# Differential attention: VectorE copies a job's values out between the two score maxima of the newest job

## The reference, cut to what matters

```python
def one_block(qi):
    s = jnp.einsum('bqhcd,bkhcd->bhcqk', qi, k).astype(jnp.float32) * scale
    p = jax.nn.softmax(s, axis=-1)
    a = p[:, :, 0] - lam * p[:, :, 1]
    return jnp.einsum('bhqk,bkhe->bqhe', a.astype(v.dtype), v)
```

## Time and profile before

| | us |
|---|---|
| runs shown (three) | 4294.61, 4308.23, 4309.19 |
| their median | 4308.23 |
| the profiled execution, its own time | 4303.0 |
| its span in the trace | 4300.9 |
| first scores of the heads start at | 3423.48 |
| last "square" of the heads ends at | 3579.61 |

### The profile page before, as it was taken

One profiled execution on the slowest core, in us unless ns is written; L12 is line 12 of the kernel. 1 busy time (PEld: TensorE's weight loads), 2 busy tenths in 40 slices (PEclk: granted clock), 3 DMA queues, 4 the chain that ended last, 5 costly groups with the idle time before them and its releaser, 6 DMA issues. The chain is left out here.

```text
span 4300.9 us, 75825 instructions
## 1 busy us (share of the span) xinstructions
PE 3759.1 (87%) x32214; PEld 2095.4 (49%) x32214; DVE 1533.8 (36%) x3723; ACT 1372.6 (32%) x2940; POOL 201.0 (5%) x193
## 2 busy tenths in 40 slices
PE   7998778777776998998988979999969988799997
PEld 4554566666665544564666533333345454333332
DVE  3011666666664103452256231111132183211112
ACT  2102334344433113442546222222235262222222
POOL 0000000000000001100200000000012000000000
PEclk9999799999998999999999989999979999899998
DMA  5223344444343110001110249999742103699996
GB/s 208 76 85 121 96 120 120 115 125 118 110 130 122 64 60 1 20 20 68 35 42 1 101 169 385 390 393 391 317 140 89 43 1 119 249 390 389 390 390 269
DMA packets 314586, 696.03 MB, mean 162 GB/s; under 512 B 169216, under 2 KB 195968, under 8 KB 289152
## 3 DMA queue, kind: packets, MB, share of 16 engines
q1 hardware_dynamic: 293024, 612.41, 40.0%
q0 software_dynamic: 14048, 53.49, 3.6%
q10 hardware_dynamic: 7168, 25.17, 1.5%
HBM read 624.94 MB, written 63.71 MB: 160 GB/s over the span
## 5 line engine op out<-in xcount | busy, mean ns | idle before, releaser
L202 PE MATMUL ps<-arena 128*128 128x512 f32 (+8 forms) x4620 | 1458.6, 479 | 95.6 <-ACT arena L1137 23.9
L202 PEld LDWEIGHTS ps<-arena 128*128 128x128 f32 (+5 forms) x4620 | 786.5, 190 | 707.1 <-issue 457.4
L2584 PE MATMUL ps<-arena 128*32 128x512 f32 x9216 | 1022.6, 596 | 31.1 <-DMA arena<-in_w 26.5
L2584 PEld LDWEIGHTS ps<-arena 128*32 128x32 f32 x9216 | 306.7, 110 | 649.0 <-issue 632.3
L620 PE MATMUL ps<-arena 64*64 64x64 f32 (+1 forms) x10624 | 463.9, 241 | 173.6 <-DVE arena L1194 62.8
L620 PEld LDWEIGHTS ps<-arena 64*64 64x64 f32 x10624 | 415.3, 146 | 255.2 <-issue 103.5
L2718 DVE COPY arena<-ps 128x384 f32<-128x384 f32 x64 | 35.7, 557 | 655.7 <-PE ps L2643 655.7
L208 PE MATMUL ps<-arena 128*128 128x128 f32 x1168 | 189.0, 296 | 83.6 <-DVE arena L3037 41.4
L2694 ACT ACTIVATE arena<-ps 96x512 f32<-96x512 f32 x64 | 38.0, 594 | 622.8 <-PE ps L2584 622.8
L208 PEld LDWEIGHTS ps<-arena 128*128 128x128 f32 x1168 | 140.3, 150 | 140.2 <-DVE arena L3037 44.9
L600 DVE SCALAR_TENSOR_TENSOR arena<-arena 128x769 f32<-128x769 f32 x48 | 45.7, 1015 | 275.9 <-PE ps L202 275.6
(11 more groups left out here) (282 smaller groups left out, 3769.4 us busy)
## 6 DMA issues: line engine op xcount, KB each, us to landing
arena<-in_w SPq DMA_DIRECT2D x192, 2048.0 KB, 30.6
arena<-in_w_mod SPq DMA_DIRECT2D x24, 2048.0 KB, 8.9
arena<-in_mod_w SPq DMA_DIRECT2D x12, 2048.0 KB, 9.4
yb<-arena ACTq DMA_DIRECT2D x64, 384.0 KB, 9.8
arena<-in_rwkv_w_in SPq DMA_DIRECT2D x8, 2048.0 KB, 10.0
arena<-rkvg SPq DMA_DIRECT2D x38, 384.0 KB, 4.2
rkvg<-arena POOLq DMA_DIRECT2D x32, 384.0 KB, 2.7
arena<-di SPq DMA_DIRECT2D x192, 64.0 KB, 2.5
```

Source lines behind the costliest of these rows:

```text
L202: ins = pe.matmul(out, l, r, start=(i == 0), stop=(i == len(pairs) - 1))
L2584: return pe.matmul(bank[32 * at:32 * at + 32, :], left[:, k, 32 * g:32 * g + 32], right[:, k, :], start=first, stop=last)
```

## The change

In DVE's order a round now has four pieces in place of three: the maximum for c = 0 of job r, "out" of job r-3, the maximum for c = 1 of job r, and "mix" of job r-1. No instruction is added or taken away, and none of ACT or PE moves. The semaphores count as before: `max` is counted by the maxima alone and `out` by "out" alone.

```diff
-        for what, n in self.rounds(((0, "max"), (3, "out"), (1, "mix"))):
+
+        for what, n in self.rounds(((0, 0), (3, "out"), (0, 1), (1, "mix"))):
...
-            elif what == "max":
-                for c in range(2):
-                    dve.wait_ge(self.scored, 2 * n + c + 1)
-                    dve.tensor_reduce(sm[:, c:c + 1], self.scores_at(n, c), AX.XY, ALU.max).then_inc(self.max, 1)
...
-            else:
+            elif what == "out":
                 dve.wait_ge(self.valued, n + 1)
                 dve.tensor_scalar(self.rows(n), self.values_at(n), sm[:, 4:5], None, ALU.mult).then_inc(self.out, 1)
+            else:
+                c = what
+                dve.wait_ge(self.scored, 2 * n + c + 1)
+                dve.tensor_reduce(sm[:, c:c + 1], self.scores_at(n, c), AX.XY, ALU.max).then_inc(self.max, 1)
```

More of the change, by code:

```diff
@@ L2505, in dve @@
                 dve.scalar_tensor_tensor(P0, P1, sm[:, 6:7], P0, ALU.mult, ALU.add).then_inc(self.mixed, 1)
-            elif what == "max":
-                for c in range(2):
-                    dve.wait_ge(self.scored, 2 * n + c + 1)
-                    dve.tensor_reduce(sm[:, c:c + 1], self.scores_at(n, c), AX.XY, ALU.max).then_inc(self.max, 1)
-                    dve.wait_ge(self.max, 4 * n + 2 * c + 1)
-                    dve.tensor_scalar(sm[:, c:c + 1], sm[:, c:c + 1], -self.SCALE, None, ALU.mult).then_inc(self.max, 1)
-            else:
+            elif what == "out":
                 dve.wait_ge(self.valued, n + 1)
                 dve.tensor_scalar(self.rows(n), self.values_at(n), sm[:, 4:5], None, ALU.mult).then_inc(self.out, 1)
+            else:
+                c = what
+                dve.wait_ge(self.scored, 2 * n + c + 1)
+                dve.tensor_reduce(sm[:, c:c + 1], self.scores_at(n, c), AX.XY, ALU.max).then_inc(self.max, 1)
+                dve.wait_ge(self.max, 4 * n + 2 * c + 1)
+                dve.tensor_scalar(sm[:, c:c + 1], sm[:, c:c + 1], -self.SCALE, None, ALU.mult).then_inc(self.max, 1)
     def over(self, e):
```

## The result

| | us |
|---|---|
| before, median of 20 runs | 4306.28 (4294.61 to 4314.16) |
| changed, median of 20 runs | 4319.62 (4309.90 to 4334.23) |
| ratio, with its 95% interval | 1.0035 (1.0026 to 1.0045) |
| span of the profiled execution, changed | 4321.8 |

The changed kernel is slower by 0.35%, some 15 us. The forecast was 4321 us.

A forecast was written before the change was run, and what follows sets the result against it. The prediction took a once-a-round loop through DVE, ACT and PE as the bound, 5.10 us against 4.58: -0.1 (first rounds) + 14.0 (27 rounds) + 1.3 (last) = 15.3 us slower, on 4305.6 giving 4321 us, range 4307 to 4331.

The forecast's parts named there:

- The loop: Out, second maximum, scaling, second exponential, square, turned, value, out, once a round: 5.10 us against 4.58, 14.0 lost in 27 rounds.
- The wait for "out" goes, and a longer one comes: PE no longer waits for "out" but about 1.0 us for ACT's copy before each value; DVE idles 1.2 before "out".
- the prediction's round of DVE, 3.89: DVE's instructions of one round added up without any wait: 3.89 us, shorter than the 5.10 us loop.
- Scores done before the copy: PE finishes its scores 2.49 us after "out" starts; the copy is ready for value only after 3.46.
- First rounds: Start of the heads: first "out" moves from 3438.79 to 3438.48; the second "out" comes 0.08 us earlier.
- Last rounds: After the last regular "out", the next value starts 3.46 us later instead of 2.15: 1.3 us lost.
- The clock rival: PE's clock falls in the rounds, each of 27 values pays 0.62 us, 16.7 us on top: 4338 us; chance 0.08.
- The faster rival: The copy does not bind and PE's loop sets the round: 15.4 us faster, 4290 us; chance 0.06.
- The level: Starting time to which the loss is added: middle of four executions, 4305.6 us, giving 4321 us.
- the band of 0.5%: What a measurement can tell from no change, 21.5 us; chance within it 0.76, slower 0.19, faster 0.05.
- The upper bound: A round costs between 0.48 and 0.60 us more, the whole 14 to 18 us; with the clock's placement 13 to 19.
- the rule of the Trainium skill: A Vector operation starts only once the previous one's pipe is empty: 27 x 0.08 = 2.2 us more; not adopted.

The follow-up runs named there:

- The 7.24 and 6.17 us rounds of one kernel: Kernel before, with DVE's "out" moved ahead of both maxima and ACT's order unchanged: median 4366.57 us, ratio 1.0152.
- 7.88 and 6.55 of another: Changed kernel, with DVE's "mix" also moved ahead of the second maximum and ACT's order unchanged: median 4369.41 us, ratio 1.0159.

## Why the prediction was right, and where it was off

- **The loop.** Its seven steps were added to 5.10 us from rows of the kernel before; the changed kernel has 5.11 or 5.12 in each of 27 rounds. Its steps as the round at 3495.45 shows them are 0.27, 0.98, 0.18, 0.90, 0.29, 0.85 and 1.64, none more than 0.01 from its term. The copy between the exponentials opens it, square ahead of them shortens it by its 0.29, mix in it lengthens it. This is shown, not only argued.
- **The wait for "out" goes, and a longer one comes.** PE waits 1.0 us for the copy ahead of each value (predicted 1.0), DVE 1.22 ahead of "out" (predicted 1.2). The 1.2 was right by two errors that cancel: the prediction's round of DVE, 3.89, holds "mix" with its whole 1.02 where the next instruction starts after 0.93 or 0.94, and the last scaling with 0.07 where the idle time begins only after its whole 0.15. The weight loads' wait for "out" did not go altogether, as I had written: 9.6 us are left, 0.35 each. Most of that lies beside PE's matmuls of the first half, and since PE waits for the copy later in the round, it costs nothing.
- **Scores done before the copy.** In the round shown the scores end at 3497.89 (3496.33 and 1.56), 2.44 us after "out" started (predicted 2.49), before the copy has even begun; the value starts at 3498.92, 3.47 after "out" (predicted 3.46), and waits for line 2478 alone.
- **First rounds.** Relative to the first maximum the first "out" came at 13.34 us, where 13.65 was before: 0.31 gained, as worked out. The gain left at the second "out" is 0.06 (predicted 0.08).
- **Last rounds.** From the last regular "out" to the next value: 3.47 us (3587.48 to 3590.95), predicted 3.46, before 2.15. The value behind it took 1.60, not 2.22, because in this execution the low clock did not fall there; that is 0.6 us in this step and 0.4 in the next, the reason why the heads lost 14.6 and not 15.6 us. So two deviations partly cancel in the sum, 15.3 against 14.6: the rounds lost 14.3 where it had 14.0, and the absent low clock, which the prediction had named in its bounds, gave 1.0 back.
- **The clock rival.** It did not happen in the changed kernel: 1.00 in the round looked at and in all of the stretch from 3450 to 3580 us:

```profile
3496.33:3501.44 5.11, 3.97 (x27) 2.69 (x26) 3.75 (x9) 2.97 (x7) 0.00 (x0) 1.00 0.00 0
3450.00:3580.00 130.00, 101.13 (x661) 68.17 (x660) 95.86 (x205) 75.59 (x180) 0.00 (x0) 1.00 0.00 1
```

  These are stretches of the changed kernel, columns as in the earlier trace rows. Other kernels did fall into it. With PE idle for 2.5 us ahead of each value, or twice, 1.5 and 0.5 us, in a round of 6.2, the clock fell again and again. The changed kernel, with 1.0 us in 5.11, stayed clear of it in both of its traces. What decides is not shown: its one idle time of 2.52 us ahead of a value, in the tail, left the clock at 1.00, and one of 2.23 us in the same place of the kernel with square ahead was followed by 0.51.
- **The faster rival.** It was 4290 us on the condition that the copy is done when the scores end. With that condition made true by the order on ACT the ratio is 0.9965, which on 4306 is 4291 us.
- **The level.** I added the loss to the middle of four executions, 4305.6; the median of 20 is 4306.3. The measured difference of the medians is 13.3 us, the ratio stands for 15; the forecast of 15.3 us is inside its interval of 11 to 19. That is 0.35%, inside the band of 0.5%, as the likeliest case had it; but with 20 runs of each kernel the interval (1.0026 to 1.0045) tells it from no change, which is finer than the 0.5% that the prediction took a measurement to resolve. That the middle of four executions lay within 1 us of the median of 20 is luck in part, with single executions between 4295 and 4314.
- **The upper bound.** The "14 to 18" us for the whole does not follow from its own numbers: 27 x 0.60 - 0.1 + 1.3 is 17.4. The range is hardly wider for it, and the measured loss lies far inside.
- **What the level hides.** The start of the heads differs by 6 us between the two executions compared. Had only the two spans been read, the change would have seemed to cost 21 us.

## What to carry to other kernels

Before moving an instruction up in an in-order queue, list what it waits for at its new place and what stands behind it there; then follow that second instruction to its readers, through every engine, until the chain either ends or comes back. If it comes back once a round, add up its steps: if that sum is longer than every other loop, it is the new round, whatever the removed wait was worth. And where a move costs because of an order on another engine, try both orders changed together; here each alone gave nothing or a loss, and the two gave 0.35%.

## What the runs showed of the hardware that I had not expected

- A repeated idle time of PE can cost more than itself. With 2.46 us of it ahead of each value the granted clock fell to 0.50 every fifth round, and a value took 2.93 us in place of 1.60; with 1.0 us in a round of 5.11 it never fell. The runs do not show why it falls in one round and not in the next, whose idle time is the same.
- The 7.24 and 6.17 us rounds of one kernel, and 7.88 and 6.55 of another, have the same instructions. They differ by the clock alone (0.76 and 1.00, 0.79 and 1.00 over the round), every fifth round in the second, so a mean over rounds would have given a round length that no round has.
- "Mix", 1.02 us long, put off the maximum behind it by only 0.93, and "out", 0.35 long, by 0.27: neighbours on DVE overlap by some 0.08 us. This is the measured answer to the rule of the Trainium skill weighed in the prediction ("VectorE: DVE Perf Modes", "The DRAIN you can't avoid"). The prediction gave only half of it: the same section adds that a next operation that is not held back starts earlier, and the trace agrees with that half. With 0.34 in place of 0.26 the round would have been 5.18 us, and it was 5.11.
